# A two-block transformer kernel on one core: first norm by tile, modulation sums in PSUM, and a moved group of operand sums

## The reference, cut to what matters

```
proj = xn @ w_in + b_in            # u_ssm, bgate, cgate, val, g_ssm, g_conv
y_a  = (z @ w_glu_a) * sigmoid(z @ w_glu_b)         # z = gelu(s5(u_ssm))
y_b  = (bgate * conv(cgate * val)) @ w_conv_out
h    = x + (sigmoid(g_ssm) * y_a + sigmoid(g_conv) * y_b) @ w_out
h    = h + relu(rmsnorm(h) @ w_ff1)**2 @ w_ff2
```

## Time and profile before

| what | us |
|---|---|
| median of three runs (2107.92 to 2113.22) | 2109.96 |
| the profiled execution's own time | 2110.72 |
| its span, first to last instruction | 2109.1 |
| PE busy in it (9607 matmul instructions) | 1881.1 |
| DVE, ACT, POOL busy | 1077.5, 309.3, 664.3 |

### The profile page before, as it was taken

One profiled execution on the slowest core, in us unless ns is written; L12 is line 12 of the kernel. 1 busy time (PEld: TensorE's weight loads), 2 busy tenths in 40 slices (PEclk: granted clock), 3 DMA queues, 4 the chain that ended last, 5 costly groups with the idle time before them and its releaser, 6 DMA issues.

```text
span 2109.1 us, 24750 instructions
## 1 busy us (share of the span) xinstructions
PE 1881.1 (89%) x9607; PEld 1215.3 (58%) x9607; DVE 1077.5 (51%) x1724; ACT 309.3 (15%) x571; POOL 664.3 (31%) x567
## 2 busy tenths in 40 slices
PE   5999999998998999999999999999978998775264
PEld 3433333687887888887356599998432322232132
DVE  3397968337599986535794134555242333111015
ACT  2100000010221012103112243331130000000001
POOL 1244444127336445630000466640011112222220
PEclk9999999999999999999998999999989999887687
DMA  5212121232244455531110999616079999999996
GB/s 194 80 46 74 43 77 41 79 120 80 82 165 154 160 189 183 190 120 40 40 41 16 401 413 409 273 41 240 0 276 382 368 393 393 391 406 413 410 376 278
DMA packets 117006, 425.85 MB, mean 202 GB/s; under 512 B 10328, under 2 KB 11549, under 8 KB 108573
## 3 DMA queue, kind: packets, MB, share of 16 engines
q1 hardware_dynamic: 99872, 393.86, 48.6%
q0 software_dynamic: 10240, 22.17, 3.0%
q10 hardware_dynamic: 6781, 8.27, 1.1%
HBM read 335.83 MB, written 88.43 MB: 201 GB/s over the span
## 4 chain that ended last, share of the span: by engine, by line
PE 77%; DMA 11%; DVE 6%; issue 3%; ACT 2%; ACTq 1%; DVEq 0%; POOLq 0%; POOL 0%
PE pb L863 23%; PE pb L680 21%; PE pb L1095 11%; DMA arena<-in_w_up_dram 10%; PE pb L1963 6%; PE pb L1987 3%; PE pb L1008 2%; PE pb L1944 2%; DVE arena L2994 2%; PE pb L2535 1%; PE pb L2547 1%; PE pb L1953 1%; PE pb L1101 1%; DVE arena L782 1%; PE pb L1936 1%
## 5 line engine op out<-in xcount | busy, mean ns | idle before, releaser
L680 PE MATMUL pb<-arena 128*128 128x256 f32 x2464 | 540.4, 382 | 20.6 <-DVE arena L794 6.2
L680 PEld LDWEIGHTS pb<-arena 128*128 128x128 f32 x2464 | 471.0, 192 | 90.0 <-DVE arena L794 7.0
L863 PE MATMUL pb<-arena 128*128 128x512 f32 (+1 forms) x1152 | 473.9, 571 | 1.3 <-ACT arena L854 1.3
L863 PEld LDWEIGHTS pb<-arena 128*128 128x128 f32 x1152 | 217.4, 190 | 253.5 <-issue 248.6
L1095 PE MATMUL pb<-arena 128*128 128x128 f32 x2016 | 232.0, 277 | 0.9 <-DVE arena L1635 0.9
L1095 PEld LDWEIGHTS pb<-arena 128*128 128x128 f32 x2016 | 229.1, 193 | 2.4 <-DVE arena L1635 1.3
L1963 PE MATMUL pb<-arena 128*64 128x512 f32 x640 | 155.2, 630 | 43.8 <-DMA arena<-in_w_up_dram 42.3
L2994 DVE SCALAR_TENSOR_TENSOR arena<-arena,sc 128x512 f32<-128x512 f32 x112 | 155.1, 1405 | 3.0
L1893 POOL DMA_DIRECT2D expert_rows<-arena x96 | 48.7, 507 | 313.3 <-issue 275.7
L1944 PE MATMUL pb<-arena 128*32 128x256 f32 x1088 | 84.1, 462 | 64.8 <-DMA arena<-in_w_up_dram 62.8
L1963 PEld LDWEIGHTS pb<-arena 128*64 128x64 f32 x640 | 47.0, 145 | 133.6 <-issue 133.2
(11 more groups left out here) (453 smaller groups left out, 2062.5 us busy)
## 6 DMA issues: line engine op xcount, KB each, us to landing
expert_rows<-arena SPq DMA_DIRECT2D x6, 12288.0 KB, 77.6
arena<-in_w_gate_dram SPq DMA_DIRECT2D x32, 2048.0 KB, 26.9
arena<-in_w_up_dram SPq DMA_DIRECT2D x32, 2048.0 KB, 21.9
arena<-in_w_down_dram SPq DMA_DIRECT2D x32, 2048.0 KB, 25.2
arena<-in_w_in_dram SPq DMA_DIRECT2D x16, 2048.0 KB, 8.0
arena<-in_w_ff_dram SPq DMA_DIRECT2D x16, 2048.0 KB, 8.0
arena<-in_w_mod_dram SPq DMA_DIRECT2D x12, 2048.0 KB, 8.0
arena<-in_w_out_dram SPq DMA_DIRECT2D x4, 2048.0 KB, 10.3
```

The costliest lines, as they stand in the source:

```text
L680: ins = nc.tensor.matmul(bank[:, 256 * p:256 * p + 256], l[:, j, P * p:P * p + P], r[:, j], start=(j == 0), stop=(j == nk - 1))
L863: l = nc.tensor.matmul(o, lhs[i], rhs[i], start=(i == 0), stop=(i == n - 1))
```

## The change

Four parts, and the counters that follow from them (`dve_sums` and `w_sums` count in the new order; `NORM` loses its first entry).

- **First norm by tile.** The identity is loaded first and x in four tiles. For each tile ACT squares, then takes the root with 1/D as scale and EPS as bias, DVE takes the reciprocal and multiplies the identity by it (`scaled_ident`), and PE multiplies the raw tile's eight blocks by that diagonal matrix, which scales and transposes at once, into eight banks. The gain gets a load of its own, is turned by PE and copied by ACT. The eight banks are evacuated by ACT and DVE in turn, with the gain as scale.
- **Loads.** The 15 small pieces are issued by SP after `u`, then the rest of the constants, then `cg0`, without a wait; POOL issues the loads of B and C when `u` has landed. PE turns the small pieces after the second group of `u`, and log_dt's after the third.
- **Merged rows' sums.** POOL makes the weight sums of `wo0` between those of `gb0` and `ga1`, and so those of `wo1` directly after `gb1`'s; DVE makes the four sums of `GC`. The third merge goes behind the sixth step of `gb1`.
- **Modulation rows.** The accumulator of unit m is `PB[2 * (m % 2)]` and, for the second input, the bank after it; ACT copies it to `modacc` one MLP unit later.

```diff
-    unit("-n1", "A" * 8)
+    unit("-n1", "AD" * 4)
...
-        xn = at(120, 16).rearrange("p (k d) -> p k d", k=KT)
+        gain = at(188, 1)[0:KD, 0:P]
+        gain_col = at(189, 1)[:, 0:KD]
+        scaled_ident = at(190, 2).rearrange("p (k t) -> p k t", k=KT)
+        x_tile = lambda k: a["x"][0][P * k:P * k + P]
...
-                act.dma_start(dst, src).then_inc(sem("rows_loaded"), 16)
+                sp.dma_start(dst, src).then_inc(sem("rows_loaded"), 16)
...
+        POOL_SUMS = SEVEN[:4] + ["wo0", "ga1", "gb1", "wo1"] + FF
...
+                user = {"gs0": None, "wo0": None, "ga1": "gb0", "wo1": "gb1"}.get(name, SEVEN[SEVEN.index(name) - 1])
...
-                if name == "wo0":
-                    def merged_sum(i, ins):
-                        ins.then_inc(sem("gc_sums"), 1)
-                        pool.wait_ge(sem("gc_sums"), i + 1)
-
-                    visited(pool, "gb1", "M4")
-                    pool.wait_ge(sem("merged"), 4)
-                    left_sums(TT, GC, OHS, merged_sum)
...
+        mod_parts = lambda m: [(0, 512 * m)] + ([(8, 6144 + 512 * m)] if m < 4 else [])
+        mod_jobs = lambda m: sum(len(mod_parts(i)) for i in range(m))
+        mod_bank = lambda m, i: PB[2 * (m % 2) + i]
+
+        def act_mod(act, m):
+
+            act.wait_ge(sem("mod_unit_used"), m + 1)
+            for i, (_, o) in enumerate(mod_parts(m)):
+                nc.scalar.activation(modacc[:, o:o + 512], mod_bank(m, i)[:], ACT.Copy).then_inc(sem("mod_copied"), 1)
...
-            pe.wait_ge(sem("mod_unit_used"), 12)
+            pe.wait_ge(sem("mod_copied"), mod_jobs(12))
...
-            sp.dma_start(res, a["x"][0].rearrange("(k p) d -> p k d", p=P)).then_inc(sem("x_loaded"), 16)
-            sp.dma_start(cst[:], a["consts"]).then_inc(sem("consts_loaded"), 16)
+            sp.dma_start(cst[:, 0:P], a["consts"][:, 0:P]).then_inc(sem("ident_loaded"), 16)
+            for k in range(KT):
+                sp.dma_start(res[:, k], x_tile(k)).then_inc(sem(f"x_loaded{k}"), 16)
             for n, name in enumerate(names[:-2]):
                 if n >= RSLOTS:
                     freed(sp, names[n - RSLOTS])
                 if n == 1:
-                    sp.wait_ge(sem("rows_loaded"), 16 * N_ROWS)
+                    sp_rows(sp)
+                    sp.dma_start(cst[:, P:CW], a["consts"][:, P:CW]).then_inc(sem("consts_loaded"), 16)
...
-            pe.wait_ge(sem("consts_loaded"), 16)
+            pe.wait_ge(sem("ident_loaded"), 16)
+            pe.wait_ge(sem("gain_loaded"), 16)
+            nc.tensor.transpose(PB[7][:, 0:KD], gain, ident[0:KD, 0:KD]).then_inc(sem("gain_ready"), 1)
+            for k in range(KT):
+                pe.wait_ge(sem("ident_scaled"), k + 1)
+                if k == 0:
+                    pe.wait_ge(sem("gain_ready"), 2)
+                for c in range(KD):
+                    l = nc.tensor.matmul(PB[c][:, k * P:(k + 1) * P], res[:, k, c * P:(c + 1) * P], scaled_ident[:, k],
+                                         start=True, stop=True)
+                    if k == KT - 1:
+                        l.then_inc(sem("group_done"), 1)
+            loaded(pe, "u")
+            unit_evacuated(pe, "-n1")
+            evacuated(pe, last_group["-n1"] - 2)
+            g0 = first_group["u"]
+            def u_group(i):
+                pe_group(pe, g0 + i, PB[(g0 + i) % 4][:], [W["u"][:, k, i * P:(i + 1) * P] for k in range(KD)],
+                         [xT[:, k] for k in range(KD)])
+            u_group(0)
+            u_group(1)
             pe.wait_ge(sem("rows_loaded"), 16 * N_ROWS)
             for t, n in enumerate((120, 125, 32)):
                 l = nc.tensor.transpose(PB[7][:, t * P:t * P + n], rows[0:n, t, :], ident[0:n, 0:n])
             l.then_inc(sem("cols_turned"), 1)
+            u_group(2)
             pe.wait_ge(sem("ldt_spread"), 1)
             nc.tensor.transpose(PB[7][:, 384:384 + NJ], ldtr[:], ident[0:NJ, 0:NJ]).then_inc(sem("cols_turned"), 1)
-            pe.wait_ge(sem("rows_scaled"), 0 + KT)
-            pe_turn(pe, xn, KT, "n1")
-            unit_evacuated(pe, "-n1")
-            loaded(pe, "u")
-            pe_unit_T(pe, "u", xT, KD)
+            u_group(3)
...
-            act_loads(act)
-            act.wait_ge(sem("x_loaded"), 16)
-            act_squares(act, res, KT, at(136, 4), "n1")
-            act_root(act, KT, "n1")
+            act.dma_start(gain, a["norm_mix_g"][0].rearrange("(r p) -> r p", p=P)).then_inc(sem("gain_loaded"), 16)
+            act.wait_ge(sem("eps_ready"), 1)
+            nc.scalar.activation(st[:, 6, 0:1], st[:, 7, 0:1], ACT.Sqrt).then_inc(sem("root_first"), 1)
+            act.wait_ge(sem("gain_ready"), 1)
+            nc.scalar.activation(gain_col, PB[7][:, 0:KD], ACT.Copy).then_inc(sem("gain_ready"), 1)
+            for k in range(KT):
+                act.wait_ge(sem(f"x_loaded{k}"), 16)
+                nc.scalar.activation(at(136, 4), res[:, k], ACT.Square, accum_out=st[:, 0, k:k + 1]).then_inc(sem("squares"), 1)
+                act.wait_ge(sem("squares"), SQUARES["n1"] + k + 1)
+                nc.scalar.activation(st[:, 3, k:k + 1], st[:, 0, k:k + 1], ACT.Sqrt, scale=1.0 / D,
+                                     bias=st[:, 7, 0:1]).then_inc(sem("root_first"), 1)
+            act.wait_ge(sem("gain_ready"), 2)
+            g0 = first_group["-n1"]
+            for c in range(0, KD, 2):
+                act.wait_ge(sem("group_done"), g0 + c + 1)
+                nc.scalar.activation(xT[:, c], PB[c][:], ACT.Copy, scale=gain_col[:, c:c + 1]).then_inc(sem("act_evac"), 1)
...
+                if 0 < FF.index(name) <= 12:
+                    act_mod(act, FF.index(name) - 1)
...
+            V.memset(st[:, 7, 0:1], EPS).then_inc(sem("eps_ready"), 1)
             V.memset(bbd[:], 0.0).then_inc(sem("blocks_zero"), 1)
             V.memset(cbd[:], 0.0).then_inc(sem("blocks_zero"), 1)
-            dve.wait_ge(sem("x_loaded"), 16)
-            dve_rstd(dve, ch, KT, D, "n1")
-            dve_scale_rows(dve, res, xn, KT, "n1")
-            dve.wait_ge(sem("rows_scaled"), KT)
+            dve.wait_ge(sem("ident_loaded"), 16)
+            for k in range(KT):
+                dve.wait_ge(sem("root_first"), k + 2)
+                do(V.reciprocal(st[:, 4, k:k + 1], st[:, 3, k:k + 1]))
+                TS(scaled_ident[:, k], ident, st[:, 4, k:k + 1], None, ALU.mult).then_inc(sem("ident_scaled"), 1)
+            dve.wait_ge(sem("gain_ready"), 2)
+            g0 = first_group["-n1"]
+            for c in range(1, KD, 2):
+                dve.wait_ge(sem("group_done"), g0 + c + 1)
+                TS(xT[:, c], PB[c][:], gain_col[:, c:c + 1], None, ALU.mult).then_inc(sem("dve_evac"), 1)
...
+            def last_merge_between(rows_of_mod):
+                passed.n += 1
+                if passed.n == 6:
+                    merge(1, 0)
...
-            dve_first(dve, "gb1")
-            merge(1, 0)
+            dve_first(dve, "gb1", last_merge_between)
             merge(1, 1)
+            left_sums(TT, GC, OHS, sums_of("wo"))
...
+                        if m >= 2:
+                            dve.wait_ge(sem("mod_copied"), mod_jobs(m - 1))
+                    for i, (s, o) in enumerate(mod_parts(m)):
+                        acc = mod_bank(m, i)[:]
...
+            loaded(pool, "u")
```

More of the change, by code:

```diff
@@ L561, in unit_evacuated, with sp_rows @@
             evacuated(eng, last_group[name] - 1)
-        def act_loads(act):
+        def sp_rows(sp):
             row_loads = []
@@ L648, in seven_operands, with sums_made @@
             return H1[:, 8 * (q // 2):8 * (q // 2) + 8], HS[h, q // 2], w, ws
+        DVE_SUMS = ("gs", "ga", "wo", "f1")
+        POOL_SUMS = SEVEN[:4] + ["wo0", "ga1", "gb1", "wo1"] + FF
+        def sums_made(name, step):
+            return sem("w_sums"), 4 * POOL_SUMS.index(name) + step
         def sums_before(name):
@@ L685, in pool_seven @@
             TT = nc.gpsimd.tensor_tensor
-            for n, name in enumerate(SEVEN):
-                user = SEVEN[n - 1] if n and weight_sums(name) is not OWS else None
-                if name == "wo1":
-                    user = "gb1"
+            for name in POOL_SUMS:
+                user = {"gs0": None, "wo0": None, "ga1": "gb0", "wo1": "gb1"}.get(name, SEVEN[SEVEN.index(name) - 1])
                 last = "M4" if user and by_rows(user) else "M3"
@@ L813, in program @@
         SQUARES = {"n1": 0, "n2": 4, "nc": 8, "n3": 10, "n5": 18, "n6": 22}
-        NORM = {tag: i for i, tag in enumerate(("n1", "nc", "n3", "x1", "n5", "n6"))}
+        NORM = {tag: i for i, tag in enumerate(("nc", "n3", "x1", "n5", "n6"))}
         r_sq = st[:, 2, 4:8]
@@ L833, in act_root @@
             nc.scalar.activation(st[:, 3, 0:nk], st[:, 2, 0:nk], ACT.Sqrt).then_inc(sem("roots"), 1)
-        def dve_scale_rows(dve, src, dst, nk, tag):
-            for k in range(nk):
-                nc.vector.tensor_scalar(dst[:, k], src[:, k], st[:, 4, k:k + 1], None, ALU.mult).then_inc(
```

(25 more changed lines are left out.)

16 lines of the change are left out of this document (6 added, 10 removed).

## The result

| run | median us (lowest to highest, runs) | ratio to before, 95% interval | profiled span |
|---|---|---|---|
| before | 2109.03 (2107.92 to 2113.22, 4) | 1 | 2109.1 |
| changed | 2084.63 (2082.58 to 2090.99, 4) | 0.9886 [0.986, 0.9912] | 2083.8 |

The profiled execution of the changed kernel took 2085.34 us. Its span is 25.3 us shorter than before's; the sum of the prediction was 20.5. The order of TensorE's work is the same from `u` on but for the turns of the small pieces, so the two traces can be laid beside each other at marks. The last two columns are the gain up to a mark, and what the stretch before the mark added. The prediction's terms stand beside the stretch.

A forecast was written before the change was run, and what follows sets the result against it. PE was taken as the bound, busy 1881 of 2109 us. Terms 13.7 - 5.0 + 10.5 + 1.3 = 20.5 came off 2110.72, giving 2090.2, or 2089.5 for the median; stated 2090, range 2081 to 2101.

The forecast's parts named there:

- Start: Program start up to the turn of C: u's load comes last, PE starts at 14.7 us; gain 13.7 us.
- Rival C: Start paced otherwise: loads at 254 GB/s, or first matmuls at half clock, 3 to 4 us; 2094, chance 0.12.
- What is late next: After the start: DVE's small chain and blocks of B end at 64.2, PE wants them at 71.9; cost 0.
- Merges: Before M2 of wo0: two operations of merge three wait for POOL's, about 2.1 us each; term -5.0 us.
- Rival A: Merges: DVE's and POOL's operations don't collide; time 2086, chance 0.12.
- Modulation rows: MLP: multiply-adds with one PSUM input take 0.7 us, so DVE is not late; gain 10.5 us.
- rivals B and D: MLP multiply-add on PSUM: B, stays at 1.45 us, 2102, chance 0.08; D, slower, 2142 at 2.2 us, chance 0.03.
- Second stall: PE's 2.94 us wait ending at 875.93, behind ACT's six load issues: 1.3 us comes back.
- Later stages: Expert stage: its loads wait for PE and DVE, so earlier gains move it as a whole; no term.
- Rival E: Later stages take the gain back, since the expert stage is full of loads; about 2108, chance 0.04.

The follow-up runs named there:

- e7: Changed kernel with the first norm's scale put on the rows by DVE and PE turning them by plain transposes; 2089.35 us, ratio 0.9919.
- e3: Kernel before with only the merged rows' sums part (sums on DVE, wo0's weight sums earlier, third merge behind sixth step); 2116.98 us, ratio 1.0035.
- e6: Changed kernel with GpSimd held back from wo1's weight sums until the fourth merge of GC is done; 2082.37 us, ratio 0.9885.
- e8: Changed kernel with the router's four small loads issued one unit later, behind the squares of f2_10; 2083.64 us, ratio 0.9882.
- e4: Changed kernel with the merges as before (GpSimd's sums after gb1, third merge after the last step); 2087.57 us, ratio 0.9898.
- e12: Repeat of the changed kernel with the merges as before, on another chip; 2087.9 us, ratio 0.9898.
- the second run: The changed kernel itself, measured again on a second chip; 2086.77 us, ratio 0.9904.

## Why the prediction was right, by its steps

**Start, 13.7 forecast, 10.7 measured.** The loads came as worked out: `u` by 14.9 (14.7 forecast), x as fast as ACT took it. The step that failed is "16 matmul instructions at 0.13 each ... 2.1, and 0.7 for the last evacuation ...: 13.6. So the load of `u` comes last". It counted only the last tile's rows, at the fast pace. The last diagonal was ready at 11.3 (0.5 later than forecast). PE had then begun 19 of 64 rows; the other 45 took 5.2 us, not 2.1. Two things made that queue. Seventeen rows had come at 213 instead of 111 ns, which is 1.8 us. And at 111 ns too a tile's 16 rows take 1.8 us, while ACT gives a tile each 1.4, so 1.3 us of backlog would have stood at full pace (both are estimates from these spacings). And an engine's four evacuations wait for the last tile, so they took 2.73 us in a row and ended 1.5 behind the turn, not 0.7. That makes 18.0; `e7` shows the turn's share of it.

With it went a misreading, "the trace has 1.00 over the whole start": in the kernel before the first record of the clock is at 26.27 us, so the 1.00 of the earlier trace rows is no reading, and its turn's rows follow each other every 213 ns up to that instant and every 110 ns behind it. That the slow pace is the lower of the two levels is inferred from the ratio and from the record that begins there; no record shows the lower level itself. By the Trainium skill ("TensorE: Matmul & The Clock Gate", "Wait — 56ns, not 53.3ns?") instructions of 128 columns follow each other at 106.7 ns at the one level and 55.6 at the other, a ratio of 1.9. The rows here have the same ratio at twice the length, 213 and 111. Rival C named both causes, a slow load and the first matmuls at half clock: the second came, in the turn and at about 1.8 us instead of 3 to 4, and `u` itself had neither, so its 2094 did not come.

**What is late next: right.** The small chain began at 40.42 (37.6 forecast, 2.8 late as the start was 3.4 late). DVE's blocks of B were done at 65.6, and PE turned them at 74.92 without a wait. The 10.66 of the turn of C was still 10.67 at M1 of `wo0`.

**Merges, -5.0 forecast, -5.0 measured.** Two operations waited about 2.0 us each, as forecast at 2.1. `e3` and `e6` show it alone and taken away. Rival A was `e6`: its term would be -0.8, and the wait of 6.02 against 5.04 says -1.0.

**Modulation rows, 10.5 forecast, 11.5 measured.** A multiply-add on PSUM takes 754 ns (0.7 taken, ends 0.7 and 1.45), so rivals B and D are out. It is no faster than one in SBUF by itself (over all 112 of them the median was 752 ns before, the longest 2885): what is saved is the time beside GpSimd. DVE is not late, and PE's instructions come at 0.2160 us each over the whole stretch, a little under the 0.2167 I took from a shorter one (0.4 us of the 1.0). The rest is the half clock behind the first stall, which was worth 2.2 and not 1.7.

**Second stall, 1.3 forecast, 2.4 measured.** The wait fell from 2.94 to 1.65, which is the 1.3; the half clock behind the wait, worth 1.7, did not come after the shorter one (1.00 from 850 to 880), and the next short wait grew from 0.33 to 0.90. `e8` shows the cause that the prediction named.

**Later stages, 0 forecast, 6.0 measured.** Rival E looked for a fixed point there that would take the gain back. There is none. But the granted clock moved by itself, and in this kernel it moved the right way: 5.2 of the 6.0 are in the windows above. By `e4` and `e12` it could as well have gone the other way. The sum of the steps was short by 4.8 us in the profile: this and 2.1 of the MLP with its second stall, against 3.0 too much for the start and 0.2 in the other stretches. Up to the end of the MLP's stage the traces have 19.4 against the 20.5 forecast; that this is so close is in part luck, since the start's 3.0 and the MLP's 2.1 cancel. The median of 2084.63, and 2086.77 in the second run, lie within the range for the same reason that the profile's does.

## What to carry to other kernels

A chain over tiles has to be summed as a queue on every engine in it: take the time at which the engine gets its last input and add its backlog, not the last tile's work. Two SBUF inputs beside a busy GpSimd cost a VectorE operation 0.7 us at 128 x 512 and 2.0 at 128 x 1024 here; an operand in PSUM gave the first back, and one wait that holds GpSimd the second. And a wait of a few us that is taken from TensorE is not yet won: read the granted clock over the rest of the program, stretch by stretch, before the edit is called useless or good. At the start of a program look at the spacing of equal TensorE instructions too, since the clock may have no record there and then reads 1.00.

## What the runs showed of the hardware that was not expected

- The stretches at half clock up to 1560 us are the same in two profiles of the changed kernel (0.74, 0.83, 0.83, 0.85 twice) and other in a kernel that differs only 400 us earlier (0.66, 0.83, 0.79, 0.78 in `e4`). The clock loss in them moved by up to 15 us between the kernels here (23.9 in `e6`, 38.5 in `e3`). What sets it is open.
- TensorE's first rows follow each other at 213 ns and later at 111 (before: 213 and 110), and the change comes between 10.6 and 13.2 us in the eleven profiles with the early turn, at 26.27 in the kernel before. With the early turn it sets when `u` begins, and the granted clock in the views does not show it.
- In `e7` the half clock came into the first long products (0.57 from 16 to 20 us) and cost just what the shorter turn had saved, 1.7 us. What it hung on is open: ahead of them TensorE did 32 rows and stood 2.28 us; in the changed kernel it did 64 rows and stood 1.60, in the kernel before 32 rows and 1.34, and neither lost the full clock there.
- A load of 2 KB took 5.14 us to issue from ScalarE's queue while weights were landing at 388 GB/s, and 3.12 us in `e8`, where it comes 7 us later.
